# Convolution and pool work dealt out over the parts of the first gated branch, modulation blocks spread one by one

## The reference

```python
h = rmsnorm(x, g_mix[l])
z = h @ w_in[l]                                    # 1024 x 4096
z_pool, z_c, z_b, z_v, gate_a, gate_b = ...        # 4 x 512 and 2 x 1024 columns
a = pool_mixer(z_pool, pool_group_w[l], pool_scale[l]) @ w_branch_pool[l]
b = short_conv_mixer(z_c, z_b, z_v, conv_w[l]) @ w_branch_conv[l]
m = jax.nn.sigmoid(gate_a) * a + jax.nn.sigmoid(gate_b) * b
x = x + m @ w_out[l]
h2 = rmsnorm(x, g_ffn[l])                          # then the expert retrieval
...
mod = (jax.nn.silu(c) @ ada_w + ada_b)             # second block: 1 x 6144
```

## Time and profile before

| | before |
|---|---|
| median of three runs | 2108.88 us (2108.6 to 2110.16) |
| profiled execution: its time | 2112.9 us |
| profiled execution: span of the trace | 2111.1 us, 21363 instructions |
| PE busy | 1683.1 us (80%) |
| DVE busy | 1040.4 us (49%) |
| ACT / POOL busy | 523.6 us / 651.3 us |
| DMA | 634.73 MB, mean 301 GB/s |
| mean granted clock | 0.917 of full speed |

### The profile page before, as it was taken

How to read it: one execution, slowest core, us unless ns; L and a number is a source line. 1 busy time by engine, 2 the same in 40 slices (tenths; PEclk the granted TensorE clock), 3 DMA queues, 4 the chain that set the end, 5 groups by cost and what they waited for, 6 DMA issues and landing times.

```text
span 2111.1 us, 21363 instructions
## 1 busy us (share of the span) xinstructions
PE 1683.1 (80%) x8396; PEld 1028.5 (49%) x8396; DVE 1040.4 (49%) x1885; ACT 523.6 (25%) x919; POOL 651.3 (31%) x408
## 2 busy tenths in 40 slices
PE   6898957767767777777899989999997876777765
PEld 5784922222223232226788968897894321211111
DVE  6973577766777776553562898363433100000001
ACT  4341322211221221113342535144630100000001
POOL 4330644444443443423471546143320000000000
PEclk9999989999998999998999999999997878777777
DMA  8674499999998999994343423454464799999997
GB/s 325 236 285 163 160 373 421 421 419 416 413 422 333 421 422 421 422 377 141 132 161 137 171 80 120 174 180 160 150 257 149 319 421 421 421 421 421 421 421 296
DMA packets 92243, 634.73 MB, mean 301 GB/s; under 512 B 10941, under 2 KB 13629, under 8 KB 16489
## 3 DMA queue, kind: packets, MB, share of 16 engines
q1 hardware_dynamic: 50400, 351.82, 42.6%
q0 software_dynamic: 36864, 268.45, 30.8%
q10 hardware_dynamic: 4872, 13.03, 1.7%
HBM read 632.17 MB, written 1.09 MB: 300 GB/s over the span
## 4 chain that ended last, share of the span: by engine, by line
DMA 40%; PE 39%; DVE 14%; issue 4%; ACT 3%; POOL 0%; ACTq 0%; DVEq 0%; POOLq 0%; SPq 0%
DMA t<-in_expert_uv,t 20%; DMA t<-in_eg 5%; DMA t<-in_ed 5%; DMA ring<-in_ed 5%; PE ps L504 4%; PE ps L662 4%; PE ps L506 4%; PE ps L508 4%; PE ps L538 3%; PE ps L663 3%; PE ps L677 3%; PE ps L551 3%; DMA ring<-in_eg 3%; DVE t L1781 2%; DVE t L1582 2%
## 5 line engine op out<-in xcount | busy, mean ns | idle before, releaser
L166 POOL TENSOR_TENSOR t<-ring,t 128x1024 fp32r<-128x1024 f32 x138 | 360.0, 2621 | 489.4 <-ACT t L158 489.1
L662 PE MATMUL ps<-t 128*128 128x512 f32 x512 | 286.4, 642 | 189.9 <-ACT t L1266 189.9
L2373 POOL DMA_INDIRECT t<-in_expert_uv,t x256 | 286.3, 1118 | 397.4 <-PE ps L663 375.5
L1781 DVE CUSTOM_DVE_ANT_0 t<-t 128x1024 f32<-128x1024 f32 x256 | 313.3, 1225 | 190.4 <-DMA t<-in_expert_uv,t 188.3
L158 ACT ACTIVATE t<-ring 128x1024 fp32r<-128x1024 f32 x204 | 213.1, 1056 | 246.7 <-PE ps L508 71.3
L663 PE MATMUL ps<-t 128*128 128x512 f32 x512 | 271.7, 613 | 0.0
L662 PEld LDWEIGHTS ps<-t 128*128 128x128 f32 x512 | 92.0, 198 | 359.1 <-ACT t L1266 270.3
L926 PE MATMUL ps<-t 128*32 128x512 f32 x896 | 149.5, 768 | 67.5 <-DMA t<-in_eg 24.5
L504 PE MATMUL ps<-t 128*128 128x256 f32 x992 | 145.8, 290 | 26.6 <-DVE t L166 13.0
L663 PEld LDWEIGHTS ps<-t 128*128 128x128 f32 x512 | 101.2, 198 | 130.2 <-issue 130.2
L926 PE MATMUL ps<-ring,t 128*32 128x512 f32 x640 | 115.0, 812 | 59.4 <-DMA ring<-in_ed 20.5
(11 more groups left out here) (326 smaller groups left out, 1996.0 us busy)
## 6 DMA issues: line engine op xcount, KB each, us to landing
ring<-in_w_in SPq DMA_DIRECT2D x82, 1024.0 KB, 4.9
t<-in_eg SPq DMA_DIRECT2D x40, 1024.0 KB, 26.7
t<-in_ed SPq DMA_DIRECT2D x38, 1024.0 KB, 27.3
t<-in_eu SPq DMA_DIRECT2D x34, 1024.0 KB, 27.1
ring<-in_eu SPq DMA_DIRECT2D x30, 1024.0 KB, 26.7
ring<-in_ed SPq DMA_DIRECT2D x26, 1024.0 KB, 27.0
ring<-in_ada_w SPq DMA_DIRECT2D x24, 1024.0 KB, 7.2
ring<-in_eg SPq DMA_DIRECT2D x24, 1024.0 KB, 27.1
```

The source lines that it names most:

```text
L166: e.tensor_tensor(p.lo, p.view, p.hi.bitcast(F32), ALU.subtract).then_inc(self.w.lo[eng], 1)
L662: e.matmul(sums[tt][0], s.diag[col % 4], v[:, 1024:1536], start=first, stop=last)
L1781: ins = e.tensor_tensor_reduce(out=g[:, 0:1024], in0=g[:, 0:1024], in1=s.hN[:, col // 128, :], scale=1.0, scalar=0.0, op0=ALU.mult, op1=AL ...
L2373: m.gathered[col % NGB].up(e.indirect_dma_start(out=s.gb[col % NGB], out_offset=None, in_=m.a_in["expert_uv"], in_offset=bass.IndirectOffs ...
```

## The change

It moves work between places and takes none away and adds none: the same instructions run, and DVE's, TensorE's and ACT's lists are put in another order, as is the list of DMAs.

1. DVE's convolution becomes a generator. The first product, the four groups and the last product are done one after each of the first six parts of the first branch (turns 16 to 21), behind that turn's `lo` and its modulation step. The pool differences stay where they were.
2. The modulation blocks advance by one step per part in the eight gate parts of the first branch instead of two (`pour(ada, 1 + br)`), on all three engines. A4 is then spread over the whole of the branch's gate parts, A5 and A6 fall in the second branch, and A7 is begun in the `wbc` parts and ended behind them (`pour(ada, 8)`).
3. The order of chunks changes: `wbp` now stands ahead of A5, W6 ahead of A6, W7 and `wbc` ahead of A7. The ring itself, its size and its rule are the same.

```diff
--- before.py
+++ after.py
@@ -306,14 +306,15 @@
     s.sp = Splitting(m.w, split_bufs(scope))
     s.msum, s.modr = ([ar(scope, 512) for _ in range(2)] for _ in range(2))
     s.ada = []
-    for n in range(6):
+    for n in range(8):
+        if n > 5:
+            s.ada.append(m.w.ada_pair(a["ada_w_2"][n - 1]))
         s.sp.expect(pair(a["w_in"], n), "G" if n in (0, 4) else "GV", "cols")
-        s.ada.append(m.w.ada_pair(a["ada_w_2"][n]))
-    s.sp.expect(pair(a["wbp"], 0), "GV", "wide")
-    for n in range(6, 8):
-        s.sp.expect(pair(a["w_in"], n), "GV", "cols")
-        s.ada.append(m.w.ada_pair(a["ada_w_2"][n]))
-    s.sp.expect(pair(a["wbc"], 0), "GV", "wide")
+        if n < 5:
+            s.ada.append(m.w.ada_pair(a["ada_w_2"][n]))
+        if n in (5, 7):
+            s.sp.expect(pair(a["wbp" if n == 5 else "wbc"], 0), "GV", "wide")
+    s.ada.append(m.w.ada_pair(a["ada_w_2"][7]))
     s.wo = [[m.w.raw(src) for src in halves(a["w_out"][n])] for n in range(2)]
     scope.close()
 
@@ -593,7 +594,7 @@
         part = 0
         for n in range(2):
             for _ in pe_cols(m, e, s.sp, ("gate1", br, n), s.hT):
-                pour(ada)
+                pour(ada, 1 + br)
                 if part == 4 and br == 0:
                     e.wait_ge(*m.pools.turn("pe"))
                     for half in range(2):
@@ -618,6 +619,7 @@
     e.wait_ge(*m.merged.turn("pe"))
     for tt in range(2):
         pe_raw_out(m, e, "wo1", s.mT, s.wo, tt)
+        pour(ada, 8)
     pour(ada, 100)
 
 
@@ -1194,6 +1196,8 @@
     for tt in range(2):
         e.wait_ge(*b.taken(("wo1", tt, 1)))
         act_norm(m, e, m.x, s.pf_f, (tt,))
+        if tt == 0:
+            pour(ada, 8)
     pour(ada, 100)
 
 
@@ -1626,21 +1630,30 @@
     m.v(ins)
     m.pools.up(e.tensor_tensor(s.pf, s.pf, s.pp[0][:, :, 16:272], ALU.subtract))
     e.wait_ge(*b.taken(("v", 1)))
-    m.v(e.tensor_tensor(s.cu[:, :, 2:258], s.cu[:, :, 2:258], s.zv, ALU.mult))
-    for g in range(4):
-        m.v(e.tensor_scalar(s.cy[:, g, :], s.cu[:, g, 0:256], s.cvw[:, g:g + 1], None, ALU.mult))
-        for k in (1, 2):
-            m.v(e.scalar_tensor_tensor(out=s.cy[:, g, :], in0=s.cu[:, g, k:k + 256],
-                                       scalar=s.cvw[:, 4 * k + g:4 * k + g + 1], in1=s.cy[:, g, :],
-                                       op0=ALU.mult, op1=ALU.add))
-    m.conv_y.up(e.tensor_tensor(s.cy, s.cy, s.zb, ALU.mult))
+
+    def convolved():
+        m.v(e.tensor_tensor(s.cu[:, :, 2:258], s.cu[:, :, 2:258], s.zv, ALU.mult))
+        yield
+        for g in range(4):
+            m.v(e.tensor_scalar(s.cy[:, g, :], s.cu[:, g, 0:256], s.cvw[:, g:g + 1], None, ALU.mult))
+            for k in (1, 2):
+                m.v(e.scalar_tensor_tensor(out=s.cy[:, g, :], in0=s.cu[:, g, k:k + 256],
+                                           scalar=s.cvw[:, 4 * k + g:4 * k + g + 1], in1=s.cy[:, g, :],
+                                           op0=ALU.mult, op1=ALU.add))
+            yield
+        m.conv_y.up(e.tensor_tensor(s.cy, s.cy, s.zb, ALU.mult))
+        yield
+
+    conv = convolved()
     for br in range(2):
         if br:
             e.wait_ge(*m.conv_hi.turn("dve"))
             m.conved.up(e.tensor_tensor(s.abT[1], s.cy, s.abT[0].bitcast(F32), ALU.subtract))
         for part in range(8):
             s.sp.take(e, "V")
-            pour(ada)
+            pour(ada, 1 + br)
+            if br == 0:
+                pour(conv, 1)
             if part == 4 and br == 0:
                 for half in range(2):
                     e.wait_ge(*m.pool_hi.turn("dve"))
```

## The result

The changed kernel takes 2117.74 us (median of six runs, 2115.55 to 2120.06) against 2109.36 us for the kernel before on the same chip (six runs, 2108.52 to 2110.98). The ratio is 1.0039, with a 95% interval of 1.0026 to 1.0051: 8.4 us slower, between 5.5 and 10.8. The forecast was 7.8 us slower, 2116.7 us.

The account below looks back on a forecast made before the run. It took TensorE's 9.3 us pause, waiting for a `lo` from DVE, as what stands out. A later output product (+5.9) and A7's sum (+1.9) gave 2108.9 + 7.8 = 2116.7 us, range 2105.5 to 2121.5.

Parts of the forecast that it names:

- A7's sum: A7's sum over partitions on TensorE, now in the middle of the output product and on the path: +1.9 us.
- Step 1, the pause: TensorE's pause before part 21 shrinks from 9.3 to 2.4 us and the clock stays up: 6.9 + 3.0 us gained.
- Step 2, DVE: DVE, held by POOL, uses up A4 at 114.6 instead of 106.2; TensorE ends the first branch at 121.7.
- holds by POOL: DVE is held while POOL makes a `lo`, about 2.1 us each; 4.3 for two up to A4's end.
- Step 3, W6: W6 issued from 115.0, not 106.64; TensorE pauses 3.8 us before part 28, leaving 2.7 of 6.5 us gained.
- Step 4, W7: A5's steps on DVE delay W7's chunks to 133.9 and 146.6; part 34 starts 5.5 us later, at 155.1.
- Step 5, the end: DVE's `merged` at 176.6 sets the output product's start, 176.7 instead of 170.76: +5.9 us; A6's sum costs nothing.
- rival D: Late loads delay the kernel as forecast, and clock is also lost before the output product: 2119.5 to 2122 us, 12%.
- The sum: Output product's later start, +5.9, and A7's sum, +1.9, make +7.8 us in all.
- A, that the ring keeps up: The pause before part 21 goes and W6 and W7 are issued in time: -6.8 us, 2102.1 us, 10%.
- B, hidden holds: Late loads as forecast, but POOL's holds on DVE mostly hidden: 2106.7 to 2113 us, 24%.

Follow-up runs that it names:

- changed_again: The changed kernel itself, unaltered, run once more; ratio 1.0041 against the kernel before, median 2118.33 us, stage 191.9 us.
- w7_ahead: Changed kernel with one DMA pair moved, W7 loaded ahead of A6; ratio 1.0008 against the kernel before, stage 186.3 us.
- sum_last: Changed kernel with A7's sum on TensorE behind the whole output product instead of in its middle; ratio 1.0031 against the kernel before, median 2115.93 us.
- modulation_alone: Kernel before with only single modulation steps and the changed chunk order, convolution left in one piece; ratio 1.0026 against the kernel before.
- w6_w7_ahead: Changed kernel with W6 loaded ahead of A5 and W7 ahead of A6; ratio 0.9971 against the kernel before, stage 179.3 us.
- conv_alone: Kernel before with only the convolution dealt out over the first branch's first six parts; ratio 0.9991 against the kernel before.

## Why the prediction was right, step by step

| | before | predicted | changed, +2.06 |
|---|---|---|---|
| TensorE restarts with part 21 | 103.2 | 96.35 | 96.2 |
| A4 used up, A5's second chunk issued | 106.2 (wbp) | 114.6 | 113.7 |
| W6 issued | 106.6 | 115.0 | 114.1 |
| part 28 starts | 128.2 | 125.5 | 124.6 |
| W7 issued, first and second chunk | 118.7, 120.6 | 133.9, 146.6 | 132.8, 145.7 |
| part 32 starts | 141.8 | 142.4 | 141.7 |
| part 34 starts | 149.55 | 155.1 | 154.2 |
| output product starts | 170.76 | 176.7 | 175.1 |
| A7's sum in the output product | - | +1.9 | +1.9 |

**Step 1, the pause.** Right in length: 2.25 us instead of 2.4 (the four terms ahead of the `lo` add to 3.9, where 4.0 stands). Wrong on the clock: I said it would not fall after so short a pause. In the changed kernel it did:

```profile
94.00:98.00 4.00, 3.90 (x20) 3.90 (x21) 3.93 (x5) 0.00 (x0) 2.28 (x1) 0.57 0.00 0
```

The columns are those of the earlier trace rows: the granted clock is 0.57 over these 4 us, and part 21's first two passes take 2.00 and 1.88 us instead of 1.2 and 1.1. It cost 1.5 us, and did not reach W6: from 89.08 to A4's last step DVE's rows show no wait, so that step did not depend on TensorE. In `changed_again`, after a pause of 1.67 us at the same place, the first pass took 1.22: the clock stayed up.

**Step 2, DVE.** The two holds by POOL came as priced. DVE's rows, with POOL's `lo` of parts 24 and 26 starting at 93.75 and 102.85:

```profile
92.82 1.22 DVE L166 TENSOR_TENSOR t<-ring,t 128x1024 fp32r<-128x1024 f32 x1
93.97 2.86 DVE L1586 SCALAR_TENSOR_TENSOR t<-ring,st,t 128x512 f32<-128x512 f32 x1
...
98.17 0.75 DVE L1586 SCALAR_TENSOR_TENSOR t<-ring,st,t 128x512 f32<-128x512 f32 x1
98.83 0.35 DVE L1638 TENSOR_SCALAR t<-t 128x256 f32<-128x256 f32 x1
...
102.45 3.06 DVE L1640 SCALAR_TENSOR_TENSOR t<-t 128x256 f32<-128x256 f32 x2
```

2.86 instead of 0.75 and 3.06 instead of 1.01 are two holds of 2.1. The place of a hold has its own effect: in `changed_again` the first fell one instruction later, on a `TENSOR_SCALAR` (2.49 us at 96.02), and W6 was issued 0.7 us earlier counted from the first matmul. POOL did not hold the `lo` of part 21, which was already running. The 0.9 us by which A4 ended early are mostly DVE's own work: a modulation step followed by an instruction that does not use its result takes 0.66 us to the next start (98.17 to 98.83), where I had taken the 0.78 of a chain of dependent steps.

**Step 3, W6.** The mechanism held, and the three landings after 111.6 were 4.8, 6.8 and 8.8 us, where I had 4.8, 7.3 and 9.7. TensorE's pause was 2.0 instead of 3.8: W6 came 0.9 earlier, and TensorE 0.9 later, since the `wbp` products took 13.24 us, not 11.5, with the clock down for a part of them (0.61 over 107 to 111 us), a loss that the wait swallowed. Which of the two, W6 or W7, costs what, the experiments give: with W7 freed the stage loses 6.35 us, with W6 freed as well another 7.0. Since `w7_ahead` lost 1.7 us to the clock at the output product, W7's share is rather 8.0 and W6's 5.3.

**Step 4, W7.** Held within 1.1 us at every point; the chain through two DMA landings is real, since a slow landing goes straight to the end (`sum_last`). The pause before part 34 was 2.05 instead of 5.0 only because parts 32 and 33 ran at half clock in the meantime (first pass 2.05 at 139.68); in `changed_again`, with the clock up there, it was 4.7. Part 34 starts when it is loaded, either way.

**Step 5, the end.** The term of the sum that was too large: +5.9 for the output product's start, of which +4.3 came (175.06 against 170.76). It was also given to the wrong engine. DVE's last stretch, from the `lo` of part 35 to `merged`, was 19.7 us instead of 20.4, and A4's 0.9 us came through, so `merged` came at 172.73:

```profile
153.05 0.48 DVE L1583 TENSOR_SCALAR t<-ring,st 128x512 f32<-128x512 f32 x1
...
172.04 0.69 DVE L1604 TENSOR_TENSOR t<-t 128x512 f32<-128x512 f32 x1
```

TensorE, which the prediction had done with its products 4.2 us before `merged`, was later by the 1.5 us that parts 34 and 35 lost at half clock, and its last row of A6's sum, at 172.02, ends at 173.03. So in this execution the output product waited for no DVE: its start was set 0.3 us behind `merged` by TensorE's own list, and that by the landing of W7's second chunk. The chain through W7 stays the cause, but its last piece was TensorE's, and A6's sum was not wholly at no cost. In `changed_again` the two ended together. No pause was left before the output product, and rival D's loss did not arise in this kernel, though in `w7_ahead` it did. `w_out` was hidden, as said; in `modulation_alone` alone it held the output product up, by 0.4 us. A7's sum cost its 1.9.

**The sum.** Predicted +7.8; the stage in the two profiles grew by 6.35 (4.3 to the output product's start and 2.05 behind it), the timed runs by 8.4, with an interval (5.5 to 10.8) that holds both. That the forecast lies nearer to the 8.4 than to the 6.35 is luck: the terms which it added up are those of the stage, and they were 1.5 too large. The remaining 2 us these runs do not settle. What lies behind the stage took 1907.9 us in the profile before and 1909.1 in the changed one, and between 1904.7 and 1909.1 over all ten profiled executions, so single executions scatter there by more than the 2 us in question.

**The rivals.** A, that the ring keeps up, is refuted for the changed kernel and realized by `w6_w7_ahead` at -6.1 us, for a price of -6.8. B, hidden holds, is refuted: both holds in the first branch were full. The Trainium skill (GPSIMD Engine Reference, section 8, Key points) states the contention for DVE instructions with two SBUF inputs or in a two-port mode. The trace agrees: two gate products, which read one operand from PSUM, ran beside POOL's `lo` at 122.5 to 125.7 in their usual time.

```profile
123.39 1.27 DVE L1600 TENSOR_TENSOR t<-t,ps 128x512 f32<-128x512 f32 x2
```

Up to the end of A4 no such instruction fell under a POOL `lo` (the pool halves start at 105.54, POOL had ended at 105.23), so the 1.6 us that it would have given back did not arise.

## What to carry to other kernels

Where several streams share one ring of buffers in one issue order, slowing one stream's consumption delays the loads of all that stand six places behind it: before spreading work out, write down for each load which step frees its place and which load stands in front of it. A pause at the engine that looks like the bound is worth only what the next due time behind it allows: here 7 us of pause were removed at no gain (`modulation_alone` against the changed kernel), and reordering four pairs of DMAs, with no instruction of a compute engine moved, was worth 13 us of the stage. A load whose place is freed by work of the same stage has its latency, and the latency's variation, on the path (`sum_last`: 2.5 us).

## What the runs showed of the hardware that I had not expected

**Who comes first at the start is worth 2 us.** In the kernel before, DVE's first normalization (line 1551) takes 4.57 us; in the changed kernel the same two instructions (line 1555) take 2.48, although nothing has been changed in front of them. POOL's first `lo` starts beside them in both:

```profile
12.15 4.57 DVE L1551 SCALAR_TENSOR_TENSOR t<-x,st,g 128x1024 f32<-128x1024 f32 x2
13.24 5.69 POOL L166 TENSOR_TENSOR t<-ring,t 128x1024 fp32r<-128x1024 f32 x2 [12.28 <-ACT t L158]
```

```profile
12.19 2.48 DVE L1555 SCALAR_TENSOR_TENSOR t<-x,st,g 128x1024 f32<-128x1024 f32 x2
13.47 3.42 POOL L166 TENSOR_TENSOR t<-ring,t 128x1024 fp32r<-128x1024 f32 x1 [12.50 <-ACT t L158]
```

When POOL comes at 13.24, DVE's second instruction is held by it; when it comes at 13.47, DVE goes first and POOL is the one stretched (3.42 instead of about 2.5). Counted from the start of DVE's first instruction, POOL came 1.06 to 1.22 us later in the six executions in which DVE was held, and 1.24 to 1.39 us later in the four in which it was not. TensorE's first matmul moves from 14.81 to 16.87. Over the ten profiled executions it was at 14.8 to 15.0 in four and at 16.9 to 17.0 in six, with no relation to the edits: the changed kernel was once in the one group and once in the other. So two executions of one kernel can be 2.1 us apart from their start on, a quarter of the 8.4 us by which the change slowed the kernel, and single profiles have to be compared from a point behind it. Whether the timed runs fall into two such groups was not tested.

**The clock after short pauses is not the same twice.** At one and the same place, before part 21, it was down after a pause of 2.25 us (changed) and up after one of 1.67 us (changed_again) and after 3.31 us (conv_alone, first pass 1.22). Before the output product it was down after 1.06 us (w7_ahead) and up after 1.60 us (before, both halves 27.73 us together). In this range a pause's length alone did not tell what it costs.
